# Reordering the seven products of each block of an MLP, and moving the splits of its row sums

## The chip, the cores and the metric

One core of a Trainium2 chip runs the whole kernel. The metric is the device time of one execution in microseconds (us); lower is better. TensorE is called PE in the profile, its weight loads PEld, VectorE is DVE, ScalarE is ACT, GpSimd is POOL, and SP is the engine whose queue issues most of the transfers.

## The reference, cut to what matters

Two layers, each with a token mixer, a cross-attention into 256 memory tokens and a squared-ReLU MLP, each wrapped in norms. x is 512 tokens by 1024 channels, all in float32. Only the MLP is touched by the change, together with the seam from the first layer to the second:

```python
h = rms_norm(x, g[4])                                  # 512 x 1024
f = jnp.square(jax.nn.relu(h @ w_up[l])) @ w_down[l]   # 1024 -> 4096 -> 1024
x = x + rms_norm(f, g[5])
```

## The kernel before, in words

**Three passes.** To keep float32 accuracy each product is made of three passes: both operands are split into a high part (`hi`, rounded) and a low part (`lo`, the rest), and PE computes hi·hi, hi·lo and lo·hi (`three_passes`, lines 893 to 895). The high part is a copy on ACT, the low part a subtraction on DVE. So every block of weights, 128 x 2048 numbers on chip, passes ACT (`product_hi`, L1358, output `w_hi`) and then DVE (`product_lo`, L1749, output `w_lo`) before PE can use it, and the rows that meet it pass ACT (`rows_hi`, L1413, `a_hi`) and DVE (`rows_lo`, L1792, `a_lo`). There are two slots for split weights and three for split rows (`ASLOTS`). A slot of weights is free once the product two places earlier has ended on PE (`tile_done`).

**Seven products for eight.** The MLP goes in four groups g of 1024 hidden channels. Each group has an up part (x to hidden) and a down part (hidden to output). Both are 2 x 2 block products done with seven multiplications instead of eight, except the up part of group 0, which is done plainly (`first_up`, `second_up`). The up products are p1 to p7, the down products m1 to m7. Operands are named by quarters of the weights: product 1 and 7 use quarter a, 2 uses b, 6 and 3 use f, 5 uses c, 4 uses d. c, a and f are sums of quarters, made by transfers that add in memory (`add_by_dma`, L2453, issued by POOL) and by one sum on POOL (`second_sum`, L2468). On the side of the rows, the up part uses sums t1 to t4 of quadrants of h (`quadrant_sum_of`, and split by `quadrant_split_hi`, L1367, and `quadrant_split_lo`), made once a layer. The down part uses the hidden blocks a11, a21, a12, a22 and sums of them: m1 uses a11, m2 a12, m5 the difference a5 = a21 - a11 (made by POOL, `rows_difference`, L2478), m6 then a11 overwritten by a5 - a22 (`late_sum`, L1803, DVE), m7 and m4 further late sums.

**Where results lie.** Products of the up part accumulate in the banks `proj[0:2]` (p1, p6, p7, p4, one on top of the other) and `proj[2:4]` (p2, then p5, p3). Between two products the running value must be read out: by ACT (`up_copy`, L1381, after p1, p6, p5), by DVE (`up_add`, L1827, after p2, p7, p3), and by ACT with a ReLU after p4 (`up_square`, L1390). a11, a22 and a12 are squared by ACT (L1398), a21 by DVE (L1835). In the down part m1, m6, m7, m4 use `proj[2:4]`, m3 `proj[0:2]`, m5 and m2 have banks in `work`, where they accumulate over all groups and are added to the output by `gather` (L1876, L1878) in the last group. The other sums into the output `ys` are `add_product` (L1855 to L1859).

**The order of the work.** Nothing is scheduled at run time: each engine runs its own list in order, and waits on counters of the others. The order of products on PE is written out in two tuples, and the lists of ACT (`first_up`, `later_up`, `down` under `block.scalar`), DVE (the same names under `block.vector`), POOL and SP (`load_phase`) are written by hand to fit:

```python
PRODUCTS = ("m1", "m5", "m6", "m2", "m7", "m3", "m4")
UPS = ("p1", "p2", "p6", "p5", "p7", "p3", "p4")
```

Five buffers of raw weights rotate through the quarters (`phase_buffers`): a phase is one up or down part, and SP loads the quarters c, a, b, d of the next phase as soon as products of the present one have had their weights split. At the end of the last group of layer 0, PE also turns (transposes) the normed memory tokens for layer 1 (`MEMORY_TURNS`), ACT and DVE split what is turned (L1442, L1948), and DVE and ACT start the norm of the MLP's output (`e3_squares` L1427 and L1435, `gain` L1922, `update` L1930).

Of the kernel before, what the change touches and what calls it, by code (L numbers as in the profile page):

```python
# [11 lines left out]
ALU = mybir.AluOpType  # L12
# [55 lines left out]
PRODUCTS = ("m1", "m5", "m6", "m2", "m7", "m3", "m4")  # L68
UPS = ("p1", "p2", "p6", "p5", "p7", "p3", "p4")
# [48 lines left out]
def phase_buffers():  # L118

    phases = [{"c": 2, "a": 3, "f": 4, "b": 0, "d": 1}]  # L120
    while len(phases) < PHASES:
        old = phases[-1]
        first, second = ("c", "b") if len(phases) % 2 else ("b", "c")
        phases.append({"c": old[first], "a": old[second], "f": old["a"], "b": old["f"], "d": old["d"]})
    return phases
# [13 lines left out]

OPERAND = {"1": "a", "2": "b", "6": "f", "5": "c", "7": "a", "3": "f", "4": "d"}  # L140
# [10 lines left out]
MEMORY_TURNS = (("m7", 1), ("m3", 0))  # L151
# [200 lines left out]
QUADRANTS = ("t3", "t1", "t2", "t4")  # L352
# [57 lines left out]
def trunk(nc, x, mem, positions, norm_g, w_in, sgu_w, sgu_b, sgu_ln_g, sgu_ln_b, w_out,  # L410
          x_wq, x_wkv, x_wo, w_up, w_down, c_ident, c_logcount, c_upper, c_decay, c_inv, out):
    weights = {"w_in": w_in, "w_out": w_out, "x_wq": x_wq, "x_wkv": x_wkv, "x_wo": x_wo}
    with ExitStack() as ctx:
# [322 lines left out]
        def _(sp):  # L736
# [45 lines left out]
            def load_phase(l, p):  # L782

                up_last = p % 2 == 0
                split_of(l, p - 1, "2" if up_last else "5")
                sp.wait_ge(t_made, nth(t_made, l, SUM_STEPS * p))
                load_quarter(l, p, "c")
                split_of(l, p - 1, "5" if up_last else "2")
                load_quarter(l, p, "a")
                split_of(l, p - 1, "3")  # L790
                load_quarter(l, p, "b")
                split_of(l, p - 1, "4")
                load_quarter(l, p, "d")
# [19 lines left out]
            for l in range(DEPTH):  # L813
# [48 lines left out]
                if l < DEPTH - 1:  # L862
                    for kb in range(KB):
                        split_of(l, PHASES - 1, "4" if kb else "7")
# [13 lines left out]
        def _(pe):  # L878
# [345 lines left out]
            def product(l, g, name):  # L1224
# [8 lines left out]
                for i in range(2):  # L1233
# [19 lines left out]
                    if (name, i) in MEMORY_TURNS and g == GROUPS - 1 and l < DEPTH - 1:  # L1253
                        t = MEMORY_TURNS.index((name, i))
                        pe.wait_ge(gathered, nth(gathered, l, 4 + 2 * t))
                        turn_normed(l, "memk", t)
# [76 lines left out]
        def _(act):  # L1333
# [269 lines left out]
            def first_up(l):  # L1603
# [5 lines left out]
                quadrant_split_hi(l, "t3")  # L1609
                quadrant_split_hi(l, "t1")  # L1610
                product_hi(l, 0, "m1")
                relu_up(l, 4)
                relu_up(l, 5)
                quadrant_split_hi(l, "t2")
                relu_up(l, 6)
                relu_up(l, 7)
                rows_hi(l, 0, "m5")
                product_hi(l, 0, "m5")
                quadrant_split_hi(l, "t4")

            def later_up(l, g):
# [8 lines left out]
                product_hi(l, g, "p3")  # L1630
                up_copy(l, g, "p5")
                rows_hi(l, g, "m1")
                product_hi(l, g, "p4")
                up_square(l, g, "a22")
                product_hi(l, g, "m1")
                rows_hi(l, g, "m5")
                product_hi(l, g, "m5")
                up_square(l, g, "a12")

            def down(l, g):  # L1640
# [3 lines left out]
                product_hi(l, g, "m2")  # L1644
                rows_hi(l, g, "m2")
                product_hi(l, g, "m7")
                rows_hi(l, g, "m7")
                product_hi(l, g, "m3")
                rows_hi(l, g, "m3")
                product_hi(l, g, "m4")  # L1650
# [7 lines left out]
                if l < DEPTH - 1:  # L1658
                    act.wait_ge(w_lo_done, nth(w_lo_done, l, product_block(g, "m3") + 1))
# [72 lines left out]
        def _(dve):  # L1732
# [19 lines left out]
            def quadrant_sum_of(l, name):  # L1752

                for i in range(2):
# [6 lines left out]
                    elif name == "t4":  # L1761

                        dve.wait_ge(tile_done, nth(tile_done, l, done(group_block(0, KB))))
                        dve.wait_ge(quadrant_sum, nth(quadrant_sum, l, QUADRANT_DONE["t2"]))
# [54 lines left out]
            def up_add(l, g, name):  # L1819
# [3 lines left out]
                for i in range(2):  # L1823
# [4 lines left out]
                                            ALU.add).then_inc(up_added, 1)  # L1828

            def square_up_rest(l, g):  # L1830

                for i in range(2):
                    part = a21[:, 2 * i:2 * i + 2]
                    dve.wait_ge(up_added, nth(up_added, l, up_add_number(g, "p3", i)))
                    nc.vector.scalar_tensor_tensor(out=part, in0=part, scalar=0.0, in1=part,  # L1835
                                                   op0=ALU.max, op1=ALU.mult).then_inc(hidden, 1)
# [381 lines left out]
            def first_up(l):  # L2218
# [7 lines left out]
                quadrant_split_lo(l, "t3")  # L2226
                quadrant_split_lo(l, "t1")
# [3 lines left out]
                square_up(l, 5)  # L2231
                quadrant_split_lo(l, "t2")
                square_up(l, 6)
                square_up(l, 7)
                rows_lo(l, 0, "m5")
                product_lo(l, 0, "m5")
                late_sum(l, 0, "m6")

            def later_up(l, g):
                product_lo(l, g, "p6")  # L2240
                if g == 1:
                    quadrant_split_lo(l, "t4")
                up_add(l, g, "p2")
                product_lo(l, g, "p5")
                product_lo(l, g, "p7")
                product_lo(l, g, "p3")
                rows_lo(l, g, "m1")
                up_add(l, g, "p7")
                product_lo(l, g, "p4")
                if g == GROUPS - 1 and l < DEPTH - 1:  # L2250
                    for t in range(MT):
                        norm_mem(l, "memk", t)
                up_add(l, g, "p3")
                square_up_rest(l, g)
                product_lo(l, g, "m1")
                rows_lo(l, g, "m5")
                product_lo(l, g, "m5")
                late_sum(l, g, "m6")

            def down(l, g):  # L2260
                last = g == GROUPS - 1
                add_both(l, g, "m1")
                product_lo(l, g, "m6")
                rows_lo(l, g, "m6")
                late_sum(l, g, "m7")
                product_lo(l, g, "m2")
                rows_lo(l, g, "m2")
                if last:
                    gather(l, "c22")
# [3 lines left out]
                if last:  # L2273
# [323 lines left out]
```

## Time and profile before

| | |
|---|---|
| median of 3 runs | 1518.08 us (1515.74 to 1522.73) |
| the profiled execution, its own time | 1519.63 us |
| span of its instructions | 1517.8 us |
| mean granted TensorE clock | 0.986 |
| PE busy | 1467.2 us, 97% of the span |
| DVE busy | 939.8 us, 62% |
| ACT busy | 701.9 us, 46% |
| POOL busy | 423.3 us, 28% |
| share of PE in the chain that ended last | 79% |

The span runs from the first to the last instruction; the profiled execution's own time lies 1.8 us above it. Busy is time in which an engine ran an instruction of its own; matmuls are pipelined, so that consecutive ones overlap in the records. In the list of waits and in the timeline, idle time ahead of an instruction is given with the instruction that released it. The MLPs take from about 413 to 765 us (layer 0) and from about 1165 us to the end (layer 1).

### The profile page before, as it was taken

What the parts mean: (1) busy time and instruction counts of PE and PEld (TensorE: products, weight loads), DVE (VectorE), ACT (ScalarE), POOL (GpSimd) and SP (SyncE); (2) the same over time, 40 slices, a digit from 0 to 9 for tenths busy, and PEclk for the clock granted to TensorE, in tenths of its full rate; (3) what the DMA queues carried; (4) which work ended last, traced back from release to release, by engine and by line L of the source; (5) the groups of instructions that cost most, each with busy time, mean ns of one, the idle gap of its engine ahead of it and who ended that gap; (6) DMA issues with size and microseconds to landing.
All of it is one profiled execution on the core that took longest, in us unless ns stands there. A gap on an engine that the chain in (4) does not pass through costs nothing.

```text
span 1517.8 us, 21108 instructions
## 1 busy us (share of the span) xinstructions
PE 1467.2 (97%) x8674; PEld 1292.0 (85%) x8674; DVE 939.8 (62%) x1087; ACT 701.9 (46%) x933; POOL 423.3 (28%) x354
## 2 busy tenths in 40 slices
PE   9999999999999989899999999999999999898987
PEld 7979998889887979889798889988888889697985
DVE  6336464746668666666892464646556786656668
ACT  6335432544435444444662453335444445544544
POOL 2001810200261443434050027112003533234341
PEclk9999999999999999999999999999999999999999
DMA  8422322520447777678463232224215368776752
GB/s 289 166 91 91 109 73 95 177 90 28 139 112 163 171 174 160 167 163 230 88 219 118 63 112 107 82 83 167 83 56 154 93 171 195 160 177 166 167 150 83
DMA packets 102592, 204.18 MB, mean 135 GB/s; under 512 B 4961, under 2 KB 21089, under 8 KB 101473
## 3 DMA queue, kind: packets, MB, share of 16 engines
q1 hardware_dynamic: 78208, 156.52, 30.4%
q0 software_dynamic: 22848, 44.05, 17.3%
q10 hardware_dynamic: 1440, 2.27, 0.4%
q8 instruction: 69, 1.13, 0.3%
q14 instruction: 27, 0.21, 0.0%
HBM read 196.52 MB, written 6.29 MB: 134 GB/s over the span
## 4 chain that ended last, share of the span: by engine, by line
PE 79%; DVE 10%; ACT 4%; issue 3%; POOL 3%; DMA 0%; ACTq 0%; POOLq 0%; DVEq 0%; SPq 0%
PE proj L893 21%; PE proj L895 21%; PE proj L894 21%; PE work L893 3%; PE work L894 3%; PE work L895 3%; DVE w_lo L1749 3%; ACT w_hi L1358 2%; PE work L922 2%; DVE w_lo L1739 1%; DVE a_lo L1792 1%; POOL a L2478 1%; PE work L958 1%; PE work L968 1%; ACT w_hi L1349 1%
## 5 line engine op out<-in xcount | busy, mean ns | idle before, releaser
L1739 DVE TENSOR_TENSOR w_lo<-w_raw,w_hi 128x2048 fp32r<-128x2048 f32 (+1 forms) x79 | 171.1, 2166 | 186.7 <-ACT w_hi L1349 186.6
L893 PE MATMUL proj<-hT_hi,w_hi 128*128 128x256 f32 (+1 forms) x800 | 258.1, 323 | 0.1
L895 PE MATMUL proj<-hT_hi,w_lo 128*128 128x256 f32 (+1 forms) x800 | 257.1, 321 | 0.0
L894 PE MATMUL proj<-hT_lo,w_hi 128*128 128x256 f32 (+1 forms) x800 | 257.0, 321 | 0.0
L893 PE MATMUL proj<-w_hi,hT_hi 128*128 128x512 f32 (+1 forms) x640 | 238.0, 372 | 1.1 <-DVE hT_lo L1998 1.1
L895 PE MATMUL proj<-w_hi,hT_lo 128*128 128x512 f32 (+1 forms) x640 | 232.1, 363 | 0.0
L894 PE MATMUL proj<-w_lo,hT_hi 128*128 128x512 f32 (+1 forms) x640 | 231.8, 362 | 0.0
L1749 DVE TENSOR_TENSOR w_lo<-w_more,w_hi 128x2048 fp32r<-128x2048 f32 x64 | 147.3, 2302 | 106.1 <-ACT w_hi L1358 106.1
L1349 ACT ACTIVATE w_hi<-w_raw 128x2048 fp32r<-128x2048 f32 (+1 forms) x79 | 139.2, 1763 | 136.1 <-PE proj L895 131.4
L1358 ACT ACTIVATE w_hi<-w_more 128x2048 fp32r<-128x2048 f32 x64 | 122.4, 1912 | 143.1 <-PE proj L895 88.8
L893 PEld LDWEIGHTS proj<-hT_hi,w_hi 128*128 128x128 f32 x800 | 152.3, 190 | 11.9 <-DVE w_lo L1739 0.4
L895 PEld LDWEIGHTS proj<-hT_hi,w_lo 128*128 128x128 f32 x800 | 152.3, 190 | 11.3
L894 PEld LDWEIGHTS proj<-hT_lo,w_hi 128*128 128x128 f32 x800 | 152.3, 190 | 11.2
L893 PE MATMUL proj<-w_hi,a_hi 128*128 128x512 f32 x320 | 127.7, 399 | 6.8 <-DVE u L1816 3.5
L893 PEld LDWEIGHTS proj<-w_hi,hT_hi 128*128 128x128 f32 x640 | 120.5, 188 | 13.7 <-DVE hT_lo L1998 1.6
L895 PEld LDWEIGHTS proj<-w_hi,hT_lo 128*128 128x128 f32 x640 | 120.1, 188 | 12.9
L894 PEld LDWEIGHTS proj<-w_lo,hT_hi 128*128 128x128 f32 x640 | 120.4, 188 | 11.8
L895 PE MATMUL proj<-w_hi,a_lo 128*128 128x512 f32 x320 | 126.2, 394 | 0.0
L894 PE MATMUL proj<-w_lo,a_hi 128*128 128x512 f32 x320 | 125.9, 393 | 0.0
L1749 DVE TENSOR_TENSOR w_lo<-w_raw,w_hi 128x2048 fp32r<-128x2048 f32 x34 | 81.1, 2387 | 31.6 <-ACT w_hi L1358 31.6
L1358 ACT ACTIVATE w_hi<-w_raw 128x2048 fp32r<-128x2048 f32 x34 | 65.1, 1915 | 70.8 <-PE proj L895 59.6
L893 PEld LDWEIGHTS proj<-w_hi,a_hi 128*128 128x128 f32 x320 | 60.9, 190 | 26.0 <-issue 11.1
(241 smaller groups left out, 2973.8 us busy)
## 6 DMA issues: line engine op xcount, KB each, us to landing
w_raw<-in_w_in_dram SPq DMA_DIRECT2D x28, 768.0 KB, 4.4
w_raw<-in_w_up_dram SPq DMA_DIRECT2D x20, 1024.0 KB, 5.4
w_more<-in_w_down_dram SPq DMA_DIRECT2D x18, 1024.0 KB, 9.0
w_more<-in_w_down_dram POOLq DMA_DIRECT2D x36, 512.0 KB, 8.0
w_raw<-in_x_wkv_dram SPq DMA_DIRECT2D x15, 1024.0 KB, 5.0
w_raw<-in_w_down_dram SPq DMA_DIRECT2D x14, 1024.0 KB, 5.2
w_more<-in_w_up_dram POOLq DMA_DIRECT2D x28, 512.0 KB, 7.5
w_more<-in_w_up_dram SPq DMA_DIRECT2D x12, 1024.0 KB, 5.3
```

What stands on the lines that cost most here:

```text
L893: nc.tensor.matmul(dst, l_hi, r_hi, start=first, stop=False, skip_group_check=more)
L894: nc.tensor.matmul(dst, l_hi, r_lo, start=False, stop=False, skip_group_check=more)
L895: return nc.tensor.matmul(dst, l_lo, r_hi, start=False, stop=last, skip_group_check=more)
L922: mm = nc.tensor.transpose(work[:, 2 * (n % 2) + half, k * P:(k + 1) * P], src[:, c * P:(c + 1) * P], ident[:])
L958: mm = nc.tensor.transpose(work[:, 2, j * P:(j + 1) * P], probs[:, u % 2, j * P:(j + 1) * P], ident[:])
L968: mm = nc.tensor.matmul(work[HD * head:HD * (head + 1), 3, place * P:(place + 1) * P], va[:, j, (h + head) * HD:(h + head + 1) * HD], prob ...
L1349: nc.scalar.activation(w_hi[:, slot, :, 0:cols], w_raw[:, raw, :, 0:cols], ACT.Copy).then_inc(w_hi_done, 1)
L1358: nc.scalar.activation(w_hi[:, slot_of(l, b)], operand(p, name), ACT.Copy).then_inc(w_hi_done, 1)
L1739: nc.vector.tensor_tensor(w_lo[:, slot, :, 0:cols], w_raw[:, raw, :, 0:cols], w_hi[:, slot, :, 0:cols].bitcast(F32), ALU.subtract).then_in ...
L1749: nc.vector.tensor_tensor(w_lo[:, slot], operand(p, name), w_hi[:, slot].bitcast(F32), ALU.subtract).then_inc(w_lo_done, 1)
L1792: nc.vector.tensor_tensor(a_lo[:, n % ASLOTS], ROWS[name], a_hi[:, n % ASLOTS].bitcast(F32), ALU.subtract).then_inc(a_lo_done, 1)
L2478: nc.gpsimd.tensor_tensor(a5[:, k], a21[:, k], a11[:, k], ALU.subtract).then_inc(s_made, 1)
```

## The change

It does four things together.

- The order of products: in the down part m2 goes second and m5 fourth (they were fourth and second); in the up part p4 goes sixth and p3 last (they were last and sixth). The rotation of the buffers (`phase_buffers`) and SP's waits (`load_phase`) follow, so that a quarter is loaded into the buffer whose product has been split.
- The lists of ACT and DVE follow. Of DVE's `later_up`, `product_lo(m1)` now stands ahead of `up_add(p3)`, and each half of a21 is squared right after its add (`square_rest`).
- The splits of the quadrant sums t1 to t4 move: on ACT out of `first_up` into the down part of group 0, on DVE out of `first_up` into the up part of group 1.
- The additions of m2 and m5 into the output in the last group (`gather`) come later: c22 after the rows of m3, c21 and c11 after those of m4 (they were after m2, m7 and m3). The two turns of the memory tokens both come after the first half of m4 (they were after the second half of m7 and the first half of m3).

```diff
-PRODUCTS = ("m1", "m5", "m6", "m2", "m7", "m3", "m4")
-UPS = ("p1", "p2", "p6", "p5", "p7", "p3", "p4")
+PRODUCTS = ("m1", "m2", "m6", "m5", "m7", "m3", "m4")
+UPS = ("p1", "p2", "p6", "p5", "p7", "p4", "p3")
...
-        first, second = ("c", "b") if len(phases) % 2 else ("b", "c")
-        phases.append({"c": old[first], "a": old[second], "f": old["a"], "b": old["f"], "d": old["d"]})
+        sixth, seventh = ("f", "d") if len(phases) % 2 else ("d", "f")
+        phases.append({"c": old["b"], "a": old["c"], "f": old["a"], "b": old[sixth], "d": old[seventh]})
...
+LAST_USE = {"b": "2", "c": "5", "a": "7", "f": "3", "d": "4"}
+def last_use(r):
+    return next(LAST_USE[q] for q in "abcdf" if BUFFERS[PHASES - 1][q] == r)
...
-MEMORY_TURNS = (("m7", 1), ("m3", 0))
+MEMORY_TURNS = ("m4", 0)
...
-QUADRANTS = ("t3", "t1", "t2", "t4")
+QUADRANTS = ("t2", "t1", "t3", "t4")
...
             def load_phase(l, p):
-                up_last = p % 2 == 0
-                split_of(l, p - 1, "2" if up_last else "5")
+                split_of(l, p - 1, "2")
+                load_quarter(l, p, "c")
+                split_of(l, p - 1, "5")
                 sp.wait_ge(t_made, nth(t_made, l, SUM_STEPS * p))
-                load_quarter(l, p, "c")
-                split_of(l, p - 1, "5" if up_last else "2")
                 load_quarter(l, p, "a")
-                split_of(l, p - 1, "3")
+                split_of(l, p - 1, "4" if p % 2 == 0 else "3")
                 load_quarter(l, p, "b")
-                split_of(l, p - 1, "4")
+                split_of(l, p - 1, "3" if p % 2 == 0 else "4")
                 load_quarter(l, p, "d")
...
-                    if (name, i) in MEMORY_TURNS and g == GROUPS - 1 and l < DEPTH - 1:
-                        t = MEMORY_TURNS.index((name, i))
-                        pe.wait_ge(gathered, nth(gathered, l, 4 + 2 * t))
-                        turn_normed(l, "memk", t)
+                    if (name, i) == MEMORY_TURNS and g == GROUPS - 1 and l < DEPTH - 1:
+                        for t in range(MT):
+                            pe.wait_ge(gathered, nth(gathered, l, 4 + 2 * t))
+                            turn_normed(l, "memk", t)
@@ ACT: def first_up(l):
                 rows_hi(l, 0, "m1")
-                quadrant_split_hi(l, "t3")
-                quadrant_split_hi(l, "t1")
                 product_hi(l, 0, "m1")
-                relu_up(l, 4)
-                relu_up(l, 5)
-                quadrant_split_hi(l, "t2")
-                relu_up(l, 6)
-                relu_up(l, 7)
-                rows_hi(l, 0, "m5")
-                product_hi(l, 0, "m5")
-                quadrant_split_hi(l, "t4")
+                for m in range(4, 8):
+                    relu_up(l, m)
+                product_hi(l, 0, "m2")
+                rows_hi(l, 0, "m2")
@@ ACT: def later_up(l, g):
-                product_hi(l, g, "p3")
+                product_hi(l, g, "p4")
                 up_copy(l, g, "p5")
                 rows_hi(l, g, "m1")
-                product_hi(l, g, "p4")
+                product_hi(l, g, "p3")
                 up_square(l, g, "a22")
                 product_hi(l, g, "m1")
-                rows_hi(l, g, "m5")
-                product_hi(l, g, "m5")
                 up_square(l, g, "a12")
+                rows_hi(l, g, "m2")
+                product_hi(l, g, "m2")
@@ ACT: def down(l, g):
                 product_hi(l, g, "m6")
                 rows_hi(l, g, "m6")
-                product_hi(l, g, "m2")
-                rows_hi(l, g, "m2")
+                if g == 0:
+                    quadrant_split_hi(l, "t2")
+                product_hi(l, g, "m5")
+                rows_hi(l, g, "m5")
+                if g == 0:
+                    quadrant_split_hi(l, "t1")
                 product_hi(l, g, "m7")
                 rows_hi(l, g, "m7")
+                if g == 0:
+                    quadrant_split_hi(l, "t3")
                 product_hi(l, g, "m3")
                 rows_hi(l, g, "m3")
+                if g == 0:
+                    quadrant_split_hi(l, "t4")
@@ DVE: def first_up(l):
-                quadrant_split_lo(l, "t3")
-                quadrant_split_lo(l, "t1")
                 product_lo(l, 0, "m1")
                 square_up(l, 4)
                 quadrant_sum_of(l, "t4")
-                square_up(l, 5)
-                quadrant_split_lo(l, "t2")
-                square_up(l, 6)
-                square_up(l, 7)
-                rows_lo(l, 0, "m5")
-                product_lo(l, 0, "m5")
+                for m in range(5, 8):
+                    square_up(l, m)
+                product_lo(l, 0, "m2")
+                rows_lo(l, 0, "m2")
                 late_sum(l, 0, "m6")
@@ DVE: def later_up(l, g):
+                if g == 1:
+                    quadrant_split_lo(l, "t2")
                 product_lo(l, g, "p6")
                 if g == 1:
-                    quadrant_split_lo(l, "t4")
+                    quadrant_split_lo(l, "t1")
                 up_add(l, g, "p2")
                 product_lo(l, g, "p5")
+                if g == 1:
+                    quadrant_split_lo(l, "t3")
                 product_lo(l, g, "p7")
-                product_lo(l, g, "p3")
+                if g == 1:
+                    quadrant_split_lo(l, "t4")
+                product_lo(l, g, "p4")
                 rows_lo(l, g, "m1")
                 up_add(l, g, "p7")
-                product_lo(l, g, "p4")
+                product_lo(l, g, "p3")
...
+                product_lo(l, g, "m1")
                 up_add(l, g, "p3")
-                square_up_rest(l, g)
-                product_lo(l, g, "m1")
-                rows_lo(l, g, "m5")
-                product_lo(l, g, "m5")
+                rows_lo(l, g, "m2")
+                product_lo(l, g, "m2")
                 late_sum(l, g, "m6")
@@ DVE: def down(l, g):
-                add_both(l, g, "m1")
+                add_product(l, g, "m1", 0)
                 product_lo(l, g, "m6")
                 rows_lo(l, g, "m6")
+                add_product(l, g, "m1", 1)
                 late_sum(l, g, "m7")
-                product_lo(l, g, "m2")
-                rows_lo(l, g, "m2")
-                if last:
-                    gather(l, "c22")
+                product_lo(l, g, "m5")
+                rows_lo(l, g, "m5")
                 add_both(l, g, "m6")
                 product_lo(l, g, "m7")
                 rows_lo(l, g, "m7")
-                if last:
-                    gather(l, "c21")
                 late_sum(l, g, "m4")
                 product_lo(l, g, "m3")
                 rows_lo(l, g, "m3")
                 if last:
-                    gather(l, "c11")
+                    gather(l, "c22")
                 add_both(l, g, "m7")
                 product_lo(l, g, "m4")
                 rows_lo(l, g, "m4")
+                if last:
+                    gather(l, "c21")
+                    gather(l, "c11")
```

## Rows read from the trace of the kernel before

**Rows 1.** Waits of PE: line waited for, us in total, times, longest.
```profile
PE work L893 <- DVE w_lo L1749: 25.3, 6, 4.7
PE proj L893 <- DVE u L1816: 3.5, 2, 2.5
...
PE proj L893 <- DVE w_lo L1739: 1.0, 1, 1.0
```

**Rows 2.** Timeline of PE, group 1 of layer 0: start, us, instruction, idle before.
```profile
551.67 0.79 PE L893 MATMUL work<-w_hi,a_hi 128*128 128x512 f32 x1 [3.97 <-DVE w_lo L1749]
```

**Rows 3.** Stretches: length, busy PE, PEld, DVE, ACT, POOL, granted clock, DMA share, GB/s.
```profile
542.07:559.93 17.86, 13.89 (x50) 10.89 (x49) 10.39 (x9) 7.64 (x7) 7.73 (x7) 0.81 0.63 128
...
714.45:734.61 20.16, 14.75 (x50) 11.34 (x49) 12.52 (x10) 7.63 (x7) 7.34 (x6) 0.83 0.35 55
...
sum 108.11, PE 80.83 PEld 63.39 DVE 64.48 ACT 45.81 POOL 44.63; mean PE 13.47 PEld 10.56 DVE 10.75 ACT 7.64 POOL 7.44
```

**Rows 4.** Stretches: group 0 of both layers; two down products; one block of up.
```profile
458.17:473.69 15.52, 12.93 (x49) 10.10 (x49) 12.43 (x14) 7.19 (x7) 2.29 (x4) 0.89 0.60 135
1209.51:1222.00 12.49, 11.32 (x49) 8.96 (x49) 11.10 (x12) 7.20 (x7) 0.93 (x2) 1.00 0.72 164
473.69:484.99 11.30, 11.16 (x48) 8.90 (x49) 9.19 (x8) 5.73 (x5) 3.97 (x4) 1.00 0.97 192
1194.78:1200.22 5.44, 5.44 (x26) 4.50 (x24) 5.41 (x6) 1.06 (x1) 4.55 (x3) 1.00 0.36 108
```

**Rows 5.** Timeline of ACT, group 1 of layer 0.
```profile
525.07 1.92 ACT L1358 ACTIVATE w_hi<-w_more 128x2048 fp32r<-128x2048 f32 x1 [3.34 <-PE proj L895]
...
546.44 1.06 ACT L1413 ACTIVATE a_hi<-a 128x1024 fp32r<-128x1024 f32 x1 [7.94 <-POOL a L2478]
547.40 1.89 ACT L1358 ACTIVATE w_hi<-w_more 128x2048 fp32r<-128x2048 f32 x1
```

**Rows 6.** Timeline of DVE, group 1 of layer 0.
```profile
530.37 1.28 DVE L1827 TENSOR_TENSOR u<-proj,u 128x512 f32<-128x512 f32 x2
...
537.12 1.49 DVE L1835 SCALAR_TENSOR_TENSOR u<-u 128x512 f32<-128x512 f32 x2
```

**Rows 7.** Timeline of POOL, group 1 of layer 0.
```profile
542.89 3.52 POOL L2478 TENSOR_TENSOR a<-u 128x512 f32<-128x512 f32 x2
```

**Rows 8.** Single lines over the run: ns min/median/max; then SP's loads of quarters.
```profile
L1835 DVE SCALAR_TENSOR_TENSOR u<-u x12: 676/679/1614, 537.1 to 1458.8; 128x512 f32<-128x512 f32 x12
...
L1792 DVE TENSOR_TENSOR a_lo<-u,a_hi x48: 1216/1219/2693, 439.9 to 1501.1; 128x1024 fp32r<-128x1024 f32 x48
...
DMA to landing us min/median/max: 5.0/5.5/11.8
```

**Rows 9.** Timeline of DVE, group 0 of layer 0.
```profile
451.20 2.44 DVE L1786 TENSOR_TENSOR t_lo<-t_sum,t_hi 128x1024 fp32r<-128x1024 f32 x2
...
459.95 1.29 DVE L1816 SCALAR_TENSOR_TENSOR u<-proj,u 128x512 f32<-128x512 f32 x2
```

**Rows 10.** Timeline of ACT and DVE, group 3 of layer 0.
```profile
698.55 1.92 ACT L1358 ACTIVATE w_hi<-w_more 128x2048 fp32r<-128x2048 f32 x1 [4.83 <-issue]
...
703.84 1.28 DVE L1827 TENSOR_TENSOR u<-proj,u 128x512 f32<-128x512 f32 x2
```

**Rows 11.** Timeline of ACT and DVE at the end of layer 0.
```profile
755.89 2.04 ACT L1442 ACTIVATE memT_hi<-work 128x512 fp32r<-128x512 f32 x4
...
759.16 1.92 ACT L1349 ACTIVATE w_hi<-w_raw 128x2048 fp32r<-128x2048 f32 x1
...
757.28 2.49 DVE L1948 TENSOR_TENSOR memT_lo<-work,memT_hi 128x512 fp32r<-128x512 f32 x4
...
762.07 2.30 DVE L1739 TENSOR_TENSOR w_lo<-w_raw,w_hi 128x2048 fp32r<-128x2048 f32 x1
```

**Rows 12.** Groups by line: the turns of the memory tokens on PE.
```profile
L922 PE MATMUL work<-ident,mems 128*128 128x128 f32 x32 | 4.2, 275 | 1.1 <-DVE mems L1908 1.1
```

**Rows 13.** Timeline of DVE at the end of layer 1.
```profile
1510.05 0.68 DVE L1857 TENSOR_TENSOR ys<-ys,proj 128x512 f32<-128x512 f32 x1
```

More of the change, by code:

```diff
@@ L863, in _ @@
                     for kb in range(KB):
-                        split_of(l, PHASES - 1, "4" if kb else "7")
+                        split_of(l, PHASES - 1, last_use(kb))
                         load_next(l, kb, x_wkv[l + 1:l + 2, kb * BK * P:(kb + 1) * BK * P, 0:512])
@@ L1658, in down @@
                 if l < DEPTH - 1:
-                    act.wait_ge(w_lo_done, nth(w_lo_done, l, product_block(g, "m3") + 1))
+                    for r in (2, 3):
+                        act.wait_ge(w_lo_done, nth(w_lo_done, l, product_block(g, "m" + last_use(r)) + 1))
                     for t in range(MT):
@@ L1763, in quadrant_sum_of @@
                         dve.wait_ge(tile_done, nth(tile_done, l, done(group_block(0, KB))))
-                        dve.wait_ge(quadrant_sum, nth(quadrant_sum, l, QUADRANT_DONE["t2"]))
+                        dve.wait_ge(quadrant_sum, nth(quadrant_sum, l, QUADRANT_DONE["t1"]))
                         nc.vector.tensor_tensor(t4_sum[:, :, cols], k2, t2_sum[:, :, cols], ALU.subtract).then_inc(quadrant_sum, 1)
@@ L1828, in up_add, with square_rest @@
                                             ALU.add).then_inc(up_added, 1)
[L1830 to L1836, printed above, removed]
+                    if name == "p3":
+                        square_rest(l, g, i)
+            def square_rest(l, g, i):
+                part = a21[:, 2 * i:2 * i + 2]
+                dve.wait_ge(up_added, nth(up_added, l, up_add_number(g, "p3", i)))
+                nc.vector.scalar_tensor_tensor(out=part, in0=part, scalar=0.0, in1=part,
+                                               op0=ALU.max, op1=ALU.mult).then_inc(hidden, 1)
             def add_product(l, g, name, i):
```

## The prediction

> **What bounds the kernel now.** I read the page first: PE is busy for 97% of the span and leads the chain that ended last, so time is to be had only where PE stands idle, runs at a low clock, or at the two ends where it isn't the bound. Then the waits of PE [rows 1]: almost all sits in one place, six waits, 25.3 us, for the low part of the second down product's weights; 3.5 us wait for a hidden block of group 0. The timeline shows the first of the six [rows 2]: m5 starts at 551.67, 3.97 us late. ACT tells why [rows 5]: it sat 7.94 us until POOL had made the difference a5, and only at 547.40 could it begin m5's weights, which stand behind the rows in its list. POOL began that difference at 542.89 [rows 7], after a21, the block of the product before last, had been added and squared by DVE (537.12) [rows 6]. So m5 needs the row sum with the longest history directly after m1.
>
> Then the stretches for the clock. From the end of the last up product to the start of the third down product, groups 1 to 3 of both layers, six stretches take 108.11 us; in the first the granted clock averages 0.81 [rows 3], because part of it runs at 1.2 instead of 2.4 GHz, behind the wait. Group 0 of layer 0, with a wait of 2.5 us, shows 0.89; group 0 of layer 1, with 1.0 us, shows 1.00 [rows 1, 4]. So a wait of 1 us didn't lower the clock and one of 2.5 us did. Undisturbed, one block of 24 wide matmuls takes 5.44 us and two down products 11.30 us [rows 4], 0.42 us more than 10.88: the pair is paced by ACT and DVE, since a product can start only 5.74 us (5.44 + 0.30) after the one before it has taken over PE and freed the slot, and the next then follows without a gap.
>
> **Six stretches, the main term.** After the change m2 stands behind m1. Its rows are a12, from p4, now a product earlier, and need no POOL; a5 is due two products later. I walk through group 1 of layer 0 with the durations shown.
>
> First the new wait. p4 accumulates in the banks that p7's add must read, and now follows p7 at once; p3 used other banks. DVE begins that add at 530.37, two halves of 0.64 us [rows 6]. ACT's pass at 525.07 began 0.26 us after p5's end [rows 5] and the up part ends at 542.07 [rows 3]: 17.26 us for three products, 5.76 us each, so p7 ends at 530.55. The first half is read at 531.05, so p4 starts near 531.2, 0.65 us late. In group 3 of layer 0 ACT's two DMA issues delay the whole line, the copy at 698.55 waited 4.83 us for issue, and the add comes at 703.84 [rows 10], so p4 could start at 704.6. Its place in the order was taken at about 702.85, two products before the up part's end at 714.45 [rows 3], which itself was 0.3 us behind p7: a wait of 2.06 us, 1.76 more than today. Together 5 x 0.65 + 1.76 = 5.0 us.
>
> With 0.65, p4 ends at about 536.9 and p3 at 542.7. m1's weights: ACT 1.92 us and DVE 2.3 us behind p4's end, ready at 541.4, before p3's end. Then DVE: add of p3's first half 542.0, its square 542.8, second half 543.6 (p3's end gates it), square 544.4, m2's rows 545.5, m2's weights 547.7. m1 needs the second bank only at 545.4. It ends at 542.67 + 5.44 = 548.11: m2's weights are ready 0.3 us before. ACT's share (ReLU twice and square of a12, m2's rows, some 4 passes of 1.06 us as in [rows 5]) ends at 544.9. m6 is then bound by its chain, 5.74 us behind m1's end. From the end of p3 to m6: 5.44 + 5.74 = 11.18 us. Six of them are 67.1 us, so the stretches give 108.1 - 67.1 - 5.0 = **36.0 us**, the low clock included. The other five down products keep their pace.
>
> But POOL now makes a5 (3.52 us for two halves [rows 7]) while DVE squares and splits rows; today DVE idles then. How two such passes disturb each other shows in the spread [rows 8]: the square takes 679 ns in the middle and 1614 at worst, the rows' pass 1219 and 2693. Bounds for m2: no delay (wait 0), or 0.93 + 1.47 = 2.4 us, less the 0.3 in hand, a wait of 2.1 us; m6 has 0.3 us of slack of its own, so it costs 1.8. I take 0.5 us a group, nearer the medians, since the maxima are rare: **-3.0 us** (0 to -10.8). The Trainium skill ("SBUF — State Buffer", Who interferes with whom) says that a DVE instruction with two SBUF inputs and a POOL instruction that reads SBUF exclude each other for the whole instruction, and whoever starts first wins. The maxima fit it. By this rule POOL could hold DVE in each of the six groups (1509 us, the first rival below), or lose each time and cost nothing (1488 us).
>
> **Group 0.** Before m1 DVE now skips the splits of t3 and t1 (2.44 us) and of t2 (another 1.22) that stand ahead of the hidden block at 459.95 [rows 9]; m1 follows at 458.2 without a wait. m2's weights can only start when the last up block ends and its ReLU (0.6 us) is taken: ACT 460.85, DVE 463.1, rows 464.2, so m2 at 464.3 against m1's end at 463.6; m6 at 469.9. The stretch of 15.52 us becomes 11.7. In layer 1, 12.49 becomes 11.6 [rows 4]. **+4.7 us**. The splits themselves go to ACT, 1.06 us each, in the down part, where ACT is busy for 5.73 of 11.30 us [rows 4], 2.8 us free in each product; and to DVE, 1.22 us each, in group 1's up part, where a product of 5.76 us brings one pass of 2.3 us and at times an add of 1.3. Both cover them, so nothing. If that cover were gone, at most 4 x 1.22 = 4.9 us a layer.
>
> **Clock behind the 2.06 us wait** of group 3: it is nearer to the 2.5 us that lowered the clock than to the 1.0 that didn't. (1 - 0.89) x 15.52 = **-1.7 us** [rows 4]; bounds 0 and 3.4 ((1 - 0.81) x 17.86 [rows 3]).
>
> **The seam between the layers.** Let x be the start of m4 in layer 0. DVE has four gathers of 0.62 us behind m4's rows (the turned copies run at that pitch [rows 11]); PE turns both memory tiles after half of m4, 2.8 us, and 16 transposes of 0.1 to 0.13 us [rows 12]; ACT copies at 0.5 us each to about x + 5.4, DVE splits to x + 6.1. Today that ends at 757.28 + 2.49, 0.9 us behind x, so it comes 5.2 us later. ACT has two squares behind it (1.3 us), then the weights of the next layer's first block (1.92 us; today at 759.16), DVE 2.30 us more [rows 11]: x + 11.1. PE is done with m4 at x + 7.1. It waits 3.9 us, where today there is no wait. Bounds: 2.6 us without the two squares' 1.3, 5.0 if the first square of a gathered half holds ACT longer. A wait like that of group 1 is followed by 1.7 to 3.4 us of clock loss; I take 2.5. The 1.0 us that PE waits for the third block of layer 1 today [rows 1] is swallowed. 3.9 + 2.5 - 1.0 = **-5.4 us**.
>
> **The end.** Behind m4's rows DVE works without a gap to the last updates: the add of m4's second half begins at 1510.05 [rows 13] though PE ended it about 1508. The two gathers put there are 4 x 0.62 = 2.5 us of this chain, and ACT's squares of the gathered halves, on which the first gain waits, start late by 0.9 us beyond it. **-3.3 us** (-2.4 to -4).
>
> **Transfers.** The quarters are loaded at the same places in the sequence, except that b now has to serve the second product. It is issued behind the sixth up product's low part, at 529.3, and needed by ACT at 542.9: 13.6 us, where the longest landing is 11.8 [rows 8]. No cost.
>
> **The sum.** 36.0 - 3.0 + 4.7 - 1.7 - 5.4 - 3.3 = 27.3 us. The profiled execution took 1519.6, which gives 1492.3; it lies 1.5 us above the median of the runs, 1518.1, so 1491 us.
>
> **Rivals.**
> *POOL against DVE.* Each of the six groups has the full 2.1 us wait for m2, 1.8 on m6, 7.8 us more than I take; and since 2 us is near what lowers the clock, six times 1.7 us on top: 10.2. That gives 1509; with half of the groups, 1500. For it: both engines are there at once in every group. Against: the median of twelve squares is undisturbed though POOL works beside many [rows 8]. Chance 0.18, spread over 1500 to 1509.
> *The wait only moves.* m2 stands second and inherits the wait if its rows or weights come 4 us late, for instance if ACT's passes over a12 queue behind a late weight. ACT has some 0.6 us to DVE's turn and DVE 0.3, so it takes 4 us more than any row here gives. The 36.0 becomes 0 to 8 us and the seam and end stay lost: 1518 (1511 to 1525). Chance 0.06.
> *Slower: quarter b lands late for m2.* It decides if the landing takes over 13.6 us. To be slower than before by 0.5% (7.6 us) the six groups must give back 35 us, 5.8 each, landings of 19.4 us; 11.8 is the longest of all [rows 8]. Then 1526 or more; 1530. Chance 0.04.
> *Better.* No disturbance, no low clock in group 3 nor at the seam, and 2.4 at the end: 3.0 + 1.7 + 2.5 + 0.9 less gives 1483. Chance 0.12.
>
> **The numbers.** My forecast, 1491 with 1485 to 1499 of its own, has the remaining 0.60. The range must hold 8 in 10: the forecast whole (0.60), most of the better case (0.09) and of the first rival (0.13) make 0.82 from 1481 to 1507. A measurement of this kernel can tell about 0.5%, 7.6 us, from no change. Faster by more (below 1510.5): 0.60 + 0.12 + 0.17 of the first rival = 0.89. Within: 0.07 (0.01 of the first rival, 0.06 of the wait that moves). Slower: 0.04.
>
> **What the profile after would show.** Right: no wait of PE for L1749 ahead of the second product, or under 1 us; six new waits for `u` L1827 of about 0.65 us, one of about 2; one wait of some 4 us for L1739 near the start of layer 1, followed by the one long stretch at the low clock; the mean clock up from 0.986 to about 0.995; 3 us more from the last matmul to the end. Wrong: waits of 2 us for m2 with slow squares or rows beside POOL; a low clock behind the 0.65 us waits; PE waiting for weights whose ACT pass waited for a transfer; or a seam that costs 10 us, since all of DVE's norm work hangs on it.

## The result and the profile after

The changed kernel takes 1507.30 us (1505.71 to 1509.93, 5 runs) against 1518.08 (1515.74 to 1523.35, 5 runs): ratio 0.992, 95% interval 0.990 to 0.995. It is faster, by 10.8 us where 27 were forecast. The profiled span is 1504.9 us, 12.9 less than before, at a mean granted clock of 0.992.

PE's waits after the change, in the columns of [rows 1]:

```profile
PE work L900 <- DVE w_lo L1759: 15.0, 6, 2.5
PE proj L900 <- DVE u L1837: 4.3, 6, 1.9
PE proj L900 <- DVE w_lo L1749: 3.9, 1, 3.9
...
PE work L900 <- issue: 1.1, 2, 0.6
```

The first line is the one that matters: the second down product, now m2, still waits for the low part of its weights in all six groups, 15.0 us where [rows 1] had 25.3. The other three are forecast waits: p4 behind p7's add, the seam, m2 in group 0. The six stretches from the start of m1 to the start of m6, in the columns of [rows 3]:

```profile
538.79:552.52 13.73, 11.25 (x50) 8.94 (x49) 13.56 (x12) 4.89 (x3) 6.63 (x6) 1.00 0.71 153
621.53:636.83 15.30, 12.81 (x51) 10.07 (x49) 14.77 (x12) 4.89 (x3) 8.20 (x7) 0.89 0.70 142
...
1365.39:1380.74 15.35, 12.85 (x50) 10.08 (x49) 14.78 (x12) 4.88 (x3) 8.26 (x7) 0.89 0.67 143
1449.75:1463.47 13.72, 11.22 (x50) 8.95 (x49) 13.55 (x11) 4.89 (x3) 6.63 (x6) 1.00 0.47 76
sum 85.49, PE 70.53 PEld 55.92 DVE 83.72 ACT 29.34 POOL 42.92; mean PE 11.75 PEld 9.32 DVE 13.95 ACT 4.89 POOL 7.15
```

DVE is busy by the record for 83.7 of the 85.5 us, and PE waits for it: here it has become the bound. But this busy time holds time in which DVE stood still inside its passes; without POOL's passes beside it (experiment 1) it is busy for 10.2 us of the first stretch instead of 13.6. Two of the six stretches average a clock of 0.89 and take 1.6 us more. The forecast had 67.1 us for the six, and 3.0 on top for POOL.

DVE, POOL and PE in group 1 of layer 0, as [rows 2, 6, 7]:

```profile
538.17 0.69 DVE L1846 SCALAR_TENSOR_TENSOR u<-u 128x512 f32<-128x512 f32 x1
538.99 0.69 DVE L1837 TENSOR_TENSOR u<-proj,u 128x512 f32<-128x512 f32 x1
539.72 2.71 DVE L1846 SCALAR_TENSOR_TENSOR u<-u 128x512 f32<-128x512 f32 x1
542.35 1.21 DVE L1802 TENSOR_TENSOR a_lo<-u,a_hi 128x1024 fp32r<-128x1024 f32 x1
543.49 3.37 DVE L1759 TENSOR_TENSOR w_lo<-w_raw,w_hi 128x2048 fp32r<-128x2048 f32 x1
```
```profile
539.60 2.27 POOL L2490 TENSOR_TENSOR a<-u 128x512 f32<-128x512 f32 x1
542.51 2.20 POOL L2490 TENSOR_TENSOR a<-u 128x512 f32<-128x512 f32 x1 [0.64 <-DVE u L1846]
```
```profile
546.91 0.50 PE L900 MATMUL work<-w_hi,a_hi 128*128 128x512 f32 x1 [2.48 <-DVE w_lo L1759]
```

Read the two engines against each other. POOL's first half of a5 starts at 539.60 and ends at 541.87. DVE's square of a21's second half starts 0.12 us later and ends at 542.43, 0.56 behind POOL: it stood still for nearly all of POOL's pass and did its own 0.69 us of work behind it. POOL's second half starts at 542.51, behind the rows' pass; that pass keeps its 1.21 us, and POOL ends only at 544.71. DVE's low part of the weights starts at 543.49 under it and takes 3.37 instead of 2.29. The squares over the run:

```profile
L1846 DVE SCALAR_TENSOR_TENSOR u<-u x12: 691/1700/2726, 538.2 to 1450.7; 128x512 f32<-128x512 f32 x12
```

Before, the median was 679 and the maximum 1614 [rows 8]: half of the twelve now carry POOL's pass. DVE loses 2.02 + 1.08 = 3.1 us a group; m1 ends some 0.5 us after m2's weights would have been ready, and PE waits the rest. The Trainium skill ("SBUF — State Buffer", Who interferes with whom) has the two engines exclude each other for whole instructions, whoever starts first; by that rule, this trace agrees, in both directions: DVE waits out POOL's first pass, POOL waits out DVE's rows.

The length of POOL's first half isn't DVE's doing. It is the same in the kernel before, where DVE was idle beside it:

```profile
542.89 2.27 POOL L2478 TENSOR_TENSOR a<-u 128x512 f32<-128x512 f32 x1
```

In both kernels this half stands right behind the issue of a transfer in POOL's list; in experiment 2, where it doesn't, it takes 1.29 us. So about 1.0 us of the 2.02 that the square loses may belong to the issue ahead of a5 and not to a5 itself. No run changed that alone.

The seam and the end, against [rows 11, 13]:

```profile
756.65 0.36 PE L900 MATMUL proj<-memT_hi,w_hi 128*128 128x256 f32 x1 [3.86 <-DVE w_lo L1749]
```
```profile
754.26 2.29 DVE L1749 TENSOR_TENSOR w_lo<-w_raw,w_hi 128x2048 fp32r<-128x2048 f32 x1
...
1486.06 1.28 DVE L1887 TENSOR_TENSOR ys<-ys,work 128x512 f32<-128x512 f32 x2
1487.26 1.29 DVE L1889 TENSOR_TENSOR ys<-work,ys 128x512 f32<-128x512 f32 x2
1488.46 0.69 DVE L1870 TENSOR_TENSOR ys<-proj,ys 128x512 f32<-128x512 f32 x1
1489.97 1.31 DVE L1933 TENSOR_TENSOR ys<-ys,gains 128x512 f32<-128x512 f32 x2 [0.82 <-ACT squares L1434]
```

PE waits 3.86 us at the seam, where 3.9 were forecast. At the end the two gathers (1486.06 to 1488.5) and ACT's late squares (0.82) stand in DVE's chain.

### The profile page after: what moved, and what is told of

The parts are those of the page before. It is cut to its first block and busy times, and to the rows that moved or that the text cites. A ratio compares the mean times of both kernels' runs of the same rounds, so it can differ in the third digit from the quotient of the medians.

```text
span 1504.9 us, 21108 instructions
## 1 busy us (share of the span) xinstructions
PE 1459.4 (97%) x8674; PEld 1287.3 (86%) x8674; DVE 956.9 (64%) x1087; ACT 704.4 (47%) x933; POOL 422.3 (28%) x354
## 3 DMA queue, kind: packets, MB, share of 16 engines
q10 hardware_dynamic: 1440, 2.27, 0.4%
## 5 line engine op out<-in xcount | busy, mean ns | idle before, releaser
L1365 ACT ACTIVATE w_hi<-w_more 128x2048 fp32r<-128x2048 f32 x62 | 118.8, 1916 | 171.6 <-PE proj L902 119.6
L1759 DVE TENSOR_TENSOR w_lo<-w_raw,w_hi 128x2048 fp32r<-128x2048 f32 x36 | 89.7, 2493 | 58.0 <-ACT w_hi L1365 58.0
L1365 ACT ACTIVATE w_hi<-w_raw 128x2048 fp32r<-128x2048 f32 x36 | 69.0, 1916 | 71.4 <-PE proj L902 66.6
```

Source lines behind the costliest of these rows:

```text
L1365: nc.scalar.activation(w_hi[:, slot_of(l, b)], operand(p, name), ACT.Copy).then_inc(w_hi_done, 1)
L1759: nc.vector.tensor_tensor(w_lo[:, slot], operand(p, name), w_hi[:, slot].bitcast(F32), ALU.subtract).then_inc(w_lo_done, 1)
```

## The experiments

All were timed with the kernel before on the same chip (its medians there 1517.7, 1518.8 and 1517.3 us); ratios are to it, with 95% intervals. Differences to the changed kernel compare medians from different chips, on which the kernel before lay within 1.5 us.

**1. POOL makes almost nothing of a5.** It leaves out part of the computation: 248 of 256 columns of the difference in groups 1 to 3.

```diff
-nc.gpsimd.tensor_tensor(a5[:, k], a21[:, k], a11[:, k], ALU.subtract).then_inc(s_made, 1)
+n = slice(0, 8 if g else S // 2)
+nc.gpsimd.tensor_tensor(a5[:, k, n], a21[:, k, n], a11[:, k, n], ALU.subtract).then_inc(s_made, 1)
```

> The kernel after the change, but in groups 1 to 3 POOL makes only 8 of 256 columns of a5 (the rest of a5 keeps group 0's numbers, so m5 and m6 work on other data). All counters, lists and orders stay. Theory A (POOL's two passes over a5 block DVE's square of a21 and its pass over m2's weights): the square falls from 2.7 to 0.7 us, m2's weights from 3.4 to 2.3 us, the six waits of 2.5 us for m2 vanish, m6 follows m1 by about 11.2 instead of 13.7 us, no low clock behind m2: 6 x 2.5 + 3.2 = 18 us less, about 1489 us. Theory B (DVE's list ahead of m2 is simply too long, or the weights come late from memory): the waits stay near 2.5 us and the time near 1507 us.

1487.98 us (1487.45 to 1488.65), ratio 0.980 (0.979 to 0.982): 19.3 us below the changed kernel. m2 has no wait left, and DVE's rows show why:

```profile
539.63 0.69 DVE L1846 SCALAR_TENSOR_TENSOR u<-u 128x512 f32<-128x512 f32 x1
540.24 1.22 DVE L1802 TENSOR_TENSOR a_lo<-u,a_hi 128x1024 fp32r<-128x1024 f32 x1
541.37 2.31 DVE L1759 TENSOR_TENSOR w_lo<-w_raw,w_hi 128x2048 fp32r<-128x2048 f32 x1
```

The same three passes with their own durations. The six stretches now take 67.2 us (67.1 forecast), and the time is the 1488 us that the prediction gave for passes that never meet: the gap between forecast and result is POOL's two passes. They still stand at the same place, with 16 numbers instead of 512 a partition:

```profile
539.52 4.23 POOL L2491 TENSOR_TENSOR a<-u 128x16 f32<-128x16 f32 x2
```

Now POOL is the one that waits: its second pass ends at 543.75, just behind DVE's weights (543.68), and no pass of DVE is longer. So it isn't the place alone that costs DVE, but the place together with the length of POOL's passes. The first of these passes is even recorded 0.11 us ahead of the square, which ran its 0.69 us all the same: the start in the record isn't always the moment from which POOL holds DVE.

**2. The same passes, later.** POOL waits until DVE has made m2's low part.

```diff
+pool.wait_ge(w_lo_done, nth(w_lo_done, l, product_block(g, "m2") + 1))
 for h in range(2):
```

> The kernel after the change, with POOL's passes over a5 in groups 1 to 3 held back until DVE has split m2's weights. Theory A: no wait for m2 (or under 0.3 us), the square 0.7 us; but a5 is then ready some 2.8 us later and m6, whose rows need it, starts about 1.4 us behind its place: 6 x 1.1 + 3.2 for the clock = 10 us less, about 1497 us. Theory B: m2's wait stays and m6's comes on top: 1510 us or more.

1499.06 us (1497.77 to 1502.53), ratio 0.988 (0.986 to 0.990), where 1497 was expected. The wait moved on by one product and shrank:

```profile
PE proj L900 <- issue: 10.6, 6, 1.8
```
```profile
544.73 2.54 POOL L2491 TENSOR_TENSOR a<-u 128x512 f32<-128x512 f32 x2 [3.34 <-DVE w_lo L1759]
```
```profile
546.10 2.32 DVE L1813 TENSOR_TENSOR u<-a,u 128x512 f32<-128x512 f32 x2 [1.52 <-issue]
```

With DVE idle at first, POOL takes 2.54 us for both halves. DVE's late sum needs the result, so 1.52 us of idling and 1.0 of slowing fall on m6. No stretch of low clock follows these waits.

**3. The same passes in eight pieces of 128x128.**

```diff
...
+for j in range(k.start, k.stop):
+    for c in (slice(0, P), slice(P, 2 * P)):
+        last = nc.gpsimd.tensor_tensor(a5[:, j, c], a21[:, j, c], a11[:, j, c], ALU.subtract)
+last.then_inc(s_made, 1)
```

> The kernel after the change, with each of POOL's two passes over a5 cut into four of 128x128 (groups 1 to 3); same work, same place. If a pass of POOL holds DVE off for the whole of that pass and no longer (theory A with an exclusive port), DVE is held by at most one small pass (about 0.4 us) each time: the square about 1.1 us, m2's weights 2.7, m2's wait under 1 us: about 1493 us. If the two engines share a bandwidth, or POOL's total work is what counts, nothing is won: 1505 us or more. Theory B: 1507 us.

Missed: 1515.62 us (1511.99 to 1518.28, 10 runs), ratio 0.998 (0.997 to 1.000), slower than the changed kernel; 1493 was expected, and 1505 or more if POOL's total work is what counts. The profiled execution, 1511.99, was the fastest of the ten; in it PE waits 19.1 us for m2's weights in all.

```profile
539.67 5.75 POOL L2495 TENSOR_TENSOR a<-u 128x128 f32<-128x128 f32 x8
```
```profile
539.78 2.30 DVE L1846 SCALAR_TENSOR_TENSOR u<-u 128x512 f32<-128x512 f32 x1
542.00 3.12 DVE L1802 TENSOR_TENSOR a_lo<-u,a_hi 128x1024 fp32r<-128x1024 f32 x1
545.04 2.53 DVE L1759 TENSOR_TENSOR w_lo<-w_raw,w_hi 128x2048 fp32r<-128x2048 f32 x1
```

My expectation was that a short pass holds DVE only for its own length. A square that meets a row of queued short passes loses 1.61 us, the rows 1.90, the weights 0.24: 3.75 in all, where the large passes took 3.1. DVE didn't get its turn after each short pass. The single passes in the trace show where it came in: the square ends 0.56 us behind POOL's second pass, the rows 1.09 us behind its seventh, while the third to the seventh end 0.4 us apart. Why it comes in there isn't settled by this run.

**4. The old order, with two lines of POOL's list exchanged.** The kernel before, but a5 ahead of the transfers that add into quarter a.

```diff
                     if p:
-                        add_by_dma(l, p, "a", "c")
                         if p % 2 == 0:
                             rows_difference(l, p // 2)
+                        add_by_dma(l, p, "a", "c")
```

> The kernel before the change, all orders kept, with one swap in POOL's list: the difference a5 ahead of the two transfers that add into quarter a. In the trace of before POOL waited for m1's weights and issued those transfers first (541.4), and began a5 at 542.9, though a21 was squared at about 538.6. Theory C (the 4 us wait for m5 came from POOL's list, not from m5's place): a5 ends near 542.5, m5's weights near 547.7, m5 waits under 1 us: 6 x 5 us less, clock included: 1487 us, as good as the reordering without its losses. Rival (a21 itself is too late for a product that stands second): m5 still waits 2 us or more, 1505 us or more.

1488.78 us (1487.25 to 1489.52), ratio 0.981 (0.979 to 0.982): 29 us for one line moved, more than twice what the reordering brought (1487 expected). The row that I had passed over is in the trace of before, just ahead of [rows 7]; behind it the same engine here:

```profile
541.37 2.46 POOL L2453 DMA_DIRECT2D w_more<-in_w_down_dram  x2 [3.91 <-DVE w_lo L1749]
```
```profile
536.72 4.91 POOL L2478 TENSOR_TENSOR a<-u 128x512 f32<-128x512 f32 x2 [0.68 <-issue]
541.58 2.46 POOL L2453 DMA_DIRECT2D w_more<-in_w_down_dram  x2
```

Before, POOL sat 3.91 us behind a transfer that waits for DVE to split m1's weights, and only then came to a5, whose rows had been ready since 538.6. Moved ahead, a5 begins at 536.72. It collides with DVE here too (4.91 us for its two halves, and DVE's m1 weights take 3.38), but ends at 541.6 instead of 546.4, and m5 waits 0.6 at most.

**5. DVE adds p7 ahead of the rows of m1** (the changed kernel, two lines of `later_up` exchanged).

> The kernel after the change, with DVE's add of p7 moved ahead of its pass over m1's rows. Theory (p4 waits 0.65 us because the add stands behind that pass of 1.2 us): the six waits for the hidden block vanish but for group 3 of layer 0, which falls from 1.9 to about 0.8 us, too short for a low clock: 5 x 0.65 + 1.1 + 1.6 = 6 us less, 1501 us. Rival: what PE saves there it waits again at m2, whose chain on DVE is the bound: 1507 us.

1506.37 us (1503.15 to 1509.10), ratio 0.991 (0.989 to 0.994). The five waits of p4 are gone and the sixth is 1.0 instead of 1.9, but the time is hardly less. m2's waits are the same (15.1 us in all), and now four of them, not two, are followed by the low clock, 1.6 us each; and in group 3 the add of p3 comes 1.0 us late for m1. That trace is of one execution, 1508.8 us. The four executions lie in two pairs, at 1503.5 us with a mean clock of 0.994 and at 1509 us with 0.990, so the first pair is near the 1501 that was expected. The rival's number, 1507, came out as a median of the two, and in this trace by the clock and the late add, not by longer waits at m2, the rival's reason.

**6. The gathers and turns back at early places** (the changed kernel: c11 behind the rows of m5, c22 behind those of m7, c21 behind those of m3, one turn behind each half of m3).

> The kernel after the change, with the gathers of the last group at earlier places (c11 after the rows of m5, c22 of m7, c21 of m3) and the two turns of the memory tokens after the first and the second half of m3. If the seam and the end cost what the trace of after suggests: the wait of 3.9 us at the start of layer 1 and the clock loss of 1.6 us behind it go, the old wait of 1.0 us returns, and the end is 3.2 us shorter: 7.7 us less, about 1499.5 us. Rival: the turns and gathers only move their cost into m3 and m4 (DVE's list is full there), half of it: 1503.5 us.

1502.21 us (1501.02 to 1502.56), ratio 0.989 (0.987 to 0.991): 5.1 us. The seam's wait is 0.77 us instead of 3.86, and from the last m6 to the end of the span it takes 38.2 us again, not 41.4. 7.7 us were expected. The trace shows where the rest went: four of the six waits for m2 are followed by the low clock here, two more than in the changed kernel, 1.6 us each.

**7. Only the splits moved** (the kernel before, with the splits of t1 to t4 where the change has them).

> The kernel before the change with only the splits of the quadrant sums moved, as in the change (order of products, a5, gathers as before). If that part works as read: the waits of 2.5 and 1.0 us for the hidden block in group 0 vanish, and the 1.5 us of low clock behind the first: 5 us less than before, 1513 us. Rival: the splits have lost their cover in group 0's down part or group 1's up part: no change, 1518 us.

1515.91 us (1514.65 to 1518.22, 11 runs), ratio 0.998 (0.998 to 0.999): 2.9 us. In layer 0 m1 starts at 458.14 without a wait and m5 waits 0.33. 5 us were expected, and nothing by the rival: the result lies between. PE never waits for a split that was moved; the two stretches of group 0 are 4.6 us shorter, but the six waits for m5 grew from 25.3 to 27.0 us in this trace.

**8. Experiments 4 and 7 together.**

> The kernel before the change, order of products kept, with both: the difference a5 ahead of the transfers in POOL's list (1488.8 us alone), and the splits moved. If the two are independent: 1484 us. Rival: they share what they save: 1487 us.

1486.77 us (1485.61 to 1488.20), ratio 0.979 (0.978 to 0.981): 2.0 below experiment 4. 1484 was expected if the two gains add, 1487 if they share.

**9. a5 by DVE.** The changed kernel; in groups 1 to 3 DVE makes the difference itself, between m2's weights and the late sum.

```diff
                 rows_lo(l, g, "m2")
                 product_lo(l, g, "m2")
+                for h in range(2):
...
+                    nc.vector.tensor_tensor(a5[:, k], a21[:, k], a11[:, k], ALU.subtract).then_inc(s_made, 1)
                 late_sum(l, g, "m6")
```

> The changed kernel, but in groups 1 to 3 the difference a5 is made by DVE, two halves of 128x512, right behind the low part of m2's weights, and not by POOL. My theory: what was lost in the six stretches is DVE held by POOL's pass, so with no such pass m2 has no wait, as with POOL's pass made later; there DVE's late sum for m6 still stood beside POOL and took 2.32 us instead of 1.28, 1.52 us late, and m6 waited 1.8 us in each group. Now DVE pays 1.28 us for a5 itself, the late sum ends 1.5 us sooner, and m6 waits under 0.3 us. From 1499.1 six times 1.6 less: 1490. Rival: DVE's own list is the bound of this place, each 1.28 us put into it comes out on PE; then m6 waits about 1 us more than that, and it gives 1496 or more.

1489.54 us (1488.39 to 1491.40), ratio 0.982 (0.980 to 0.984). The engine with the full list does the work and is done sooner:

```profile
541.39 1.22 DVE L1802 TENSOR_TENSOR a_lo<-u,a_hi 128x1024 fp32r<-128x1024 f32 x1
542.52 2.28 DVE L1759 TENSOR_TENSOR w_lo<-w_raw,w_hi 128x2048 fp32r<-128x2048 f32 x1
544.72 1.28 DVE L2274 TENSOR_TENSOR a<-u 128x512 f32<-128x512 f32 x2
545.93 1.28 DVE L1813 TENSOR_TENSOR u<-a,u 128x512 f32<-128x512 f32 x2
```

1.28 us on DVE replace two POOL passes that cost it 3.1; m6 waits 0.33. 1490 us was expected.

**10. Experiments 5, 6 and 9 together.**

> The changed kernel with three edits: a5 by DVE in groups 1 to 3, DVE's add of p7 ahead of the rows of m1, and the gathers and the turns of the memory tokens back at earlier places. If the gains add: from the run with a5 by DVE (1490 expected) the wait of p4 away in six groups, 0.65 x 5 + 0.9 = 4.1, and the seam and the end, 5.1: 1481. Rival: the add ahead of the rows delays m1's rows and weights and gives the 0.65 us back, as its own run showed only 1 us: 1485.

1481.02 us (1480.69 to 1481.73), ratio 0.976 (0.975 to 0.978), the best of all and the number expected; PE's longest wait in the MLPs is 1.2 us, and the mean clock 0.998. It is 8.5 us below experiment 9, where the early gathers had brought 5.1 alone. That leaves about 3.4 us for the early add, which had brought 0.9 in experiment 5; no run has the early add with a5 on DVE and nothing else, so this share is inferred.

**11. The old order, cleaned further.** Experiment 8, with the second `norm_mem` of group 3 moved behind the low part of m1's weights.

> The kernel before with POOL's list swapped (a5 ahead of the DMAs of a) and the splits moved, and with the two norms of the memory tokens in group 3 of layer 0 apart: the first stays behind the low part of p4's weights, the second moves behind that of m1's. Today both, 4.56 us, stand ahead of the add of p3 and the squares, and m1 waits 2.9 us for its weights. If this is the cause the wait goes, and 1486.8 becomes 1484. Rival: ACT's high part of m1's weights, not DVE, comes last there: no change, 1486.8.

1484.85 us (1483.70 to 1486.01), ratio 0.979 (0.977 to 0.980). The wait there falls from 2.9 to 1.8, not to zero, and DVE's pass over m1's weights still takes 3.38 us beside POOL. The step from experiment 8 is 1.9 us in the medians, and the intervals of the two ratios overlap. The reordered products (1481.0) and the old ones (1484.9) end 4 us apart: of what the order seemed to be worth, nearly all was the place of a5. The two aren't quite alike, since a5 is made by DVE in the first and by POOL in the second; the old order with a5 on DVE wasn't run.

## Why the prediction was wrong

The direction was right, and so was most of the walk through the stages; one term was far too small, and one reading of the kernel before was wrong. The time lies 0.3 us outside the range and the gain is 40% of the forecast.

| term | forecast | measured |
|---|---|---|
| six stretches, undisturbed (108.1 - 67.1) | +41.0 | +40.9 in experiment 1 (108.1 - 67.2) |
| POOL against DVE there | -3.0 | **-18.3** (85.5 - 67.2) |
| waits of p4 | -5.0 | -4.3 |
| group 0 | +4.7 | +4.6 |
| clock behind p4's wait in group 3 | -1.7 | -1.6 |
| seam | -5.4 | -4.7 |
| end | -3.3 | -3.2 |
| sum | 27.3 | 13.4, the span shows 12.9 |

**The step that failed** is the size of POOL against DVE: "I take 0.5 us a group, nearer the medians, since the maxima are rare". The term rested on the median in [rows 8], 679 ns. But a5 itself came when DVE was idle [rows 6, 7], and seven of the twelve squares met none of POOL's passes for more than 0.03 us. The other five met the end of another POOL pass, the sum of quarters of the weights (`second_sum`), and every one was longer, two by 0.2 us and three by 0.8 to 0.9. One of them with the pass that it met:

```profile
1285.40 1.60 DVE L1835 SCALAR_TENSOR_TENSOR u<-u 128x512 f32<-128x512 f32 x1
1285.14 1.30 POOL L2468 TENSOR_TENSOR w_raw<-w_more 128x512 f32<-128x512 f32 x1
```

It ends at 1287.00, 0.56 us behind POOL's pass, and the other four end as far behind theirs, just like the square in the changed kernel. So the price stood in the trace of before, and the median hid it; "the median of twelve squares is undisturbed" was no argument against the rival. The change puts the two at one place in every group, and then each DVE pass pays what is left of POOL's. The bound of 2.4 us was too low as well: it added the worst square and the worst rows' pass, but what was slowed was a square (2.02) and the weights' pass (1.08). Two waits in six also brought the low clock, 3.2 us in all. Experiment 1 gives the term back as a whole: 19.3 us. It was my first rival, at 1509 us with a chance of 0.18. That its number came so near is partly luck: it had 10.8 us of waits and 10.2 of low clock, and the trace shows 15.1 and 3.2.

**The reading of before** had a fault that the number didn't show: "m5 needs the row sum with the longest history". a5's rows were ready at 538.6; it was POOL's list that held it until 542.89 (experiment 4). Had I read what POOL did in the 4.3 us between, I would have seen that the wait needed no new order of products.

**Right as forecast:** p4's new waits (0.48 listed in five groups, 1.92 in group 3) and the low clock behind the last of them; group 0's m1 without a wait and m6 at 469.85 (469.9 forecast); the seam's wait of 3.9 us and the swallowed 1.0; the end; quarter b, for which PE and ACT never waited. PE never waited for the moved splits where they went (experiment 7).

## What to carry to other kernels

Before giving an idle engine a pass beside a busy one, look whether the two will stand at the same place in time; a median over rows of which most didn't meet is no price. Take it from the rows that did. Cost the meeting at what is left of the other engine's pass, at worst the whole of it, and compare it with what the busy engine needs to do the work itself: here 1.28 us against 3.1. And when an engine starts late on data that is ready, read the line ahead in its own list before reordering anyone else's.

## What the runs showed of the hardware

Short POOL passes issued one after the other hold DVE longer in all than two long ones: eight of 128x128 took 5.75 us and cost DVE 3.75; two of 128x512, which took 2.54 where DVE was idle at first, cost it 3.1; two of 128x16 at the same place cost it nothing. A POOL pass of 128x512 right behind the issue of a transfer took 2.27 us with DVE idle, and 1.29 in experiment 2, where it stood behind no issue. And waits of the same length don't always bring the low clock: of six waits of 2.5 us, two were followed by it in the changed kernel and four in experiment 6; a wait of 1.92 us was, in the changed kernel, and one of 2.48 us at the same place in experiment 1 wasn't; none of the six of 1.8 us in experiment 2 was.
